# A decoder layer's prologue with half sums of v and z ahead of the whole sums of q and k, and the gate rows made on VectorE alone

## The reference

```python
h = x * (1.0 + scale[:, None, :]) + shift[:, None, :]      # scale, shift, gate = silu(c) @ w_ada + b_ada
proj = h @ w_in + b_in        # sb_q, sb_k, sb_v, sb_z | ml_q, ml_k, ml_v, ml_o, ml_z, ml_i, ml_f | g_sb, g_ml
y_sb = stick_breaking_attention(sb_q, sb_k, sb_v)          # 8 heads of 64
y_sb = (y_sb * silu(sb_z)) @ w_sb_proj
mq, mk = silu(causal_depthwise_conv([ml_q, ml_k]))
hm = mlstm_chunkwise(mq, mk, ml_v, ml_i, log_sigmoid(ml_f))   # 4 heads of 128
y_ml = (head_norm(hm) * sigmoid(ml_o) * silu(ml_z)) @ w_ml_proj
y = (sigmoid(g_sb) * y_sb + sigmoid(g_ml) * y_ml) @ w_out
return layer_norm(ALPHA * x + (1.0 + gate) * y)
```

## Time and profile before

| | |
|---|---|
| median of 3 runs | 951.34 us |
| profiled execution, whole | 953.3 us |
| its span, first to last instruction | 951.6 us |
| TensorE busy | 924.0 us (97%) |
| VectorE busy | 610.9 us (64%) |
| ScalarE busy | 440.6 us (46%) |
| GpSimd busy | 167.7 us (18%) |
| mean granted TensorE clock | 0.994 |
| chain that ended last: TensorE | 92% |

### The profile page before, as it was taken

How to read it: one execution, slowest core, us unless ns; L and a number is a source line. 1 busy time by engine, 2 the same in 40 slices (tenths; PEclk the granted TensorE clock), 3 DMA queues, 4 the chain that set the end, 5 groups by cost and what they waited for, 6 DMA issues and landing times.

```text
span 951.6 us, 12863 instructions
## 1 busy us (share of the span) xinstructions
PE 924.0 (97%) x4958; PEld 756.9 (80%) x4958; DVE 610.9 (64%) x1057; ACT 440.6 (46%) x719; POOL 167.7 (18%) x118
## 2 busy tenths in 40 slices
PE   4899999999999999999999999999999999999996
PEld 3667888888888888888888888888888888878885
DVE  5838886756976748966659867534653333345997
ACT  2544766543676544665446665525742222243100
POOL 1020132230322310232311322302100000002210
PEclk9899999999999999999999999999999999999998
DMA  9921211112211113111122111127712121215232
GB/s 272 335 44 34 67 34 34 34 46 67 67 30 38 25 55 100 24 45 34 34 68 66 45 34 35 34 56 246 228 46 56 45 55 46 89 44 188 89 133 88
DMA packets 90392, 73.95 MB, mean 78 GB/s; under 512 B 4664, under 2 KB 81592, under 8 KB 90332
## 3 DMA queue, kind: packets, MB, share of 16 engines
q1 hardware_dynamic: 85380, 58.32, 22.4%
q0 software_dynamic: 2496, 8.47, 2.7%
q10 hardware_dynamic: 2456, 6.34, 1.8%
HBM read 64.59 MB, written 8.40 MB: 77 GB/s over the span
## 4 chain that ended last, share of the span: by engine, by line
PE 92%; DMA 3%; DVE 3%; SPq 1%; ACT 1%; issue 1%; DVEq 0%; ACTq 0%
PE bank L668 49%; PE bank L646 9%; PE bank L647 9%; PE bank L648 9%; PE bank L817 4%; PE bank L805 3%; DMA a_raw<-in_w_ada 2%; PE bank L792 2%; PE bank L775 2%; PE bank L794 1%; PE bank L793 1%; PE bank L829 1%; PE bank L836 1%; PE bank L840 1%; PE bank L843 1%
## 5 line engine op out<-in xcount | busy, mean ns | idle before, releaser
L668 PE MATMUL bank<-hH,wH 128*128 128x512 f32 x688 | 271.3, 394 | 3.0 <-DVE wL L1443 1.7
L668 PE MATMUL bank<-hL,wH 128*128 128x512 f32 x688 | 271.1, 394 | 0.0
L668 PE MATMUL bank<-hH,wL 128*128 128x512 f32 x688 | 271.0, 394 | 0.0
L606 POOL TENSOR_TENSOR ez<-ez,rem 128x512 f32<-128x512 f32 x72 | 134.6, 1882 | 392.5 <-DVE rem L1629 392.5
L1443 DVE SCALAR_TENSOR_TENSOR wL<-w_raw,wH 128x512 fp32r<-128x512 f32 x116 | 99.2, 859 | 109.6 <-ACT wH L1001 108.4
L668 PEld LDWEIGHTS bank<-hH,wH 128*128 128x128 f32 x688 | 129.2, 188 | 32.9 <-issue 3.7
L668 PEld LDWEIGHTS bank<-hH,wL 128*128 128x128 f32 x688 | 129.3, 188 | 28.8 <-issue 2.9
L668 PEld LDWEIGHTS bank<-hL,wH 128*128 128x128 f32 x688 | 129.3, 188 | 28.5 <-issue 2.9
L1001 ACT ACTIVATE wH<-w_raw 128x512 fp32r<-128x512 f32 x116 | 72.5, 627 | 103.7 <-PE bank L648 70.6
L1629 DVE TENSOR_TENSOR_SCAN rem<-rem,ones 128x512 f32<-128x512 f32 (+2 forms) x96 | 99.9, 1092 | 31.7 <-ACT rem L1108 31.7
L1096 ACT ACTIVATE ez<-bank 128x512 f32<-128x512 f32 x72 | 39.1, 596 | 99.8 <-PE bank L794 99.8
(11 more groups left out here) (260 smaller groups left out, 1483.6 us busy)
## 6 DMA issues: line engine op xcount, KB each, us to landing
w_raw<-in_w_in SPq DMA_DIRECT2D x104, 256.0 KB, 2.9
a_raw<-in_w_ada SPq DMA_DIRECT2D x12, 512.0 KB, 7.2
raw<-in_w_ada POOLq DMA_DIRECT2D x8, 512.0 KB, 5.3
x_in<-in_x SPq DMA_DIRECT2D x8, 512.0 KB, 4.1
out_y<-res SPq DMA_DIRECT2D x7, 512.0 KB, 2.9
x_rows<-in_x SPq DMA_DIRECT2D x3, 1024.0 KB, 10.4
raw<-in_w_out SPq DMA_DIRECT2D x10, 256.0 KB, 4.4
next_vg<-in_w_ada SPq DMA_DIRECT2D x4, 512.0 KB, 7.7
```

Of the source, the lines that this page charges most:

```text
L606: g.tensor_tensor(e, e, r, ALU.mult).then_inc(a_done[h], 1)
L668: ins = t.matmul(banks(number)[half][:], w, a, start=(r == 0), stop=(r == JOB_MM // 2 - 1))
```

## The change

The order of work in the prologue is another, in these parts:

- TensorE takes tiles 0 to 3 of h for v and z (`early`) instead of q and k. ScalarE copies the four half sums from PSUM to `part` (the place of the adaLN buffer 0), ahead of its `shifted(4)`. Then TensorE takes tiles 0 to 3 for q and k (`lower`; three of the four pieces ahead of `gate_rows(4)`), tiles 4 to 7 for q and k, and at last tiles 4 to 7 for v and z (`late`). VectorE adds bias and `part` to the late half sums (`whole_sum`) in its own order between the gates' steps. The chunks of weights are loaded in the order of `PRO`.
- The gate rows are built by VectorE without `r_e`; ScalarE takes exp(-m) straight from `r_m`.
- ScalarE casts kH and qH in the prologue, VectorE makes kL and qL there. In head 0 sig comes from `next_g` (`first_gate`), behind the evacuation of the first half of the first projection.
- `gate_columns` stands behind the scores of s = 0 of head 0; the copies into `tok` and `dec` (`token_columns`) and the columns of the head made from them (`head_tokens`) stand behind the second convolution sum of head 0.
- Buffers are laid out in another order in SBUF.

```diff
 PRE = 48
-PRO_K = 3
-PRO_CHUNKS = 2 * PRO_K
+PRO = [("if", 0), ("v", 0), ("z", 0), ("if", 1), ("q", 0), ("k", 0), ("q", 1), ("k", 1), ("v", 1), ("z", 1)]
+PRO_NAMES = ["if", "q", "k", "v", "z"]
+KH = KT // 2
 A_BUFS = 4
 BLOCKS = [[0], [1], [2, 3], [4, 5], [6, 7]]
...
@@ -659,7 +666,7 @@
                     if half == 0 and term == 0 and k % 4 == 0:
                         pe.wait_ge(wL_done, first + (k // 4 + 1))
                     if r == 0:
-                        pe.wait_ge(drained[half], number - other_banks)
+                        pe.wait_ge(drained[half], number - (1 if number == PRO_JOBS else other_banks))
                     if r == 0 and number == J_GATES + 1:
                         pe.wait_ge(at_out[half], NH * NS)
                     slot = (slot0 + k // 4) % 3
...
+                pe.wait_ge(wL_done, g + 1)
+                return [z[:, pro_slot(g)] for z in (w_proH, w_proL)] if name in "qk" else [z[:, g % 3] for z in (wH, wL)]
+            def pro_product(name, half, k, first, kt):
+                w = [z[:, k % KH] for z in pro_weights(name, k // KH)]
+                return split_product(pro_banks[name][half][:], w, (hH[:, k, halves(half)], hL[:, k, halves(half)]),
+                                     k - first, kt)
+            def early(k, names):
                 pe.wait_ge(hL_done, k + 1)
-                g = PRO_K * (k // 4) + n
-                if k % 4 == 0:
-                    pe.wait_ge(wL_done, g + 1)
-                w = [z[:, pro_slot(g), k % 4] for z in (w_proH, w_proL)]
+                for name in names:
+                    for half in range(2):
+                        ins = pro_product(name, half, k, 0, KH)
+                        if k == KH - 1:
+                            ins.then_inc(part_filled, 1)
+            def lower(name, half):
+                pe.wait_ge(part_drained, 2 * "qk".index(name) + half + 1)
+                for k in range(KH):
+                    pro_product(name, half, k, 0, KT)
+            def tile_of(k, name):
+                pe.wait_ge(hL_done, k + 1)
                 for half in range(2):
-                    ins = split_product(pro_ps[n][half], w, (hH[:, k, halves(half)], hL[:, k, halves(half)]), k, KT)
+                    ins = pro_product(name, half, k, 0, KT)
                     if k == KT - 1:
                         ins.then_inc(filled[half], 1)
+            def late(name):
+                for half in range(2):
+                    pe.wait_ge(drained[half], PRO_NAMES.index({"v": "q", "z": "k"}[name]) + 1)
+                    for k in range(KH, KT):
+                        ins = pro_product(name, half, k, KH, KH)
+                    ins.then_inc(filled[half], 1)
             def gate_columns():
                 pe.wait_ge(q_exp, 3)
+                pe.wait_ge(tok_done, 2)
                 for n in range(2):
                     pe.wait_ge(m_drained[n], M_PRO[n] - 1)
...
-            for n in range(PRO_K, PRO_JOBS):
-                project(0, 0, JOB_MM, base_job=n, other_banks=1 if n == PRO_K else 0)
-            gate_columns()
+            early(0, "v")
+            ada_columns(1)
+            early(0, "z")
+            gate_rows(0)
+            turn_x(2)
+            ada_columns(2)
+            early(1, "vz")
+            turn_x(3)
+            early(2, "vz")
+            gate_rows(2)
+            ada_columns(3)
+            turn_x(4)
+            early(3, "vz")
+            turn_x(5)
+            lower("q", 0)
+            lower("q", 1)
+            lower("k", 0)
+            gate_rows(4)
+            ada_columns(4)
+            turn_x(6)
+            lower("k", 1)
+            turn_x(7)
+            for name in "qk":
+                tile_of(4, name)
+            gate_rows(6)
+            for name in "qk":
+                tile_of(5, name)
+            for name in "qk":
+                tile_of(6, name)
+                tile_of(7, name)
+            pe.sem_inc(w_first_used, PRO_JOBS)
+            late("v")
+            late("z")
...
@@ -877,6 +930,8 @@
                         weighted_values(i, s - 3)
                         weighted_values(i, s - 2)
                     scores(i, s)
+                    if i == 0 and s == 0:
+                        gate_columns()
                     project(i, start, middle)
                     if s > 0:
...
@@ -1036,9 +1090,18 @@
             for d in range(KT):
                 shifted(d)
                 if d == 3:
-                    for g in range(3, PRO_CHUNKS):
+                    for g in range(3, 6):
                         pro_split(g)
-            for g in range(PRO_CHUNKS, PRO_CHUNKS + 3):
+                    act.wait_ge(ada_summed, BLOCK_OF[d + 1] + 1)
+                    for n, name in enumerate("vz"):
+                        for half in range(2):
+                            act.wait_ge(part_filled, 2 * n + half + 1)
+                            a.activation(part_of(name, half), pro_banks[name][half][:], ACT.Copy)\
+                                .then_inc(part_drained, 1)
+                if d == 5:
+                    for g in (6, 7):
+                        pro_split(g)
+            for g in (8, 9):
                 pro_split(g)
             act.wait_ge(params_made, 1)
...
+            act.wait_ge(bias_in, 16)
+            act.wait_ge(rows_zero, 5)
+            bias_copy(r_if[0:2 * NH, halves(0)], 0, 0, r_bias[0:2 * NH, :], pro_ps[0][0])
+            act.wait_ge(if_moved, 2)
+            bias_copy(r_if[0:2 * NH, halves(1)], 1, 0, r_bias[0:2 * NH, :], r_if[0:2 * NH, halves(1)])
+            def pair_copy(name, dst):
+                n = PRO_NAMES.index(name)
...
-                    act.wait_ge(rows_in, 16 * 4)
-                    a.activation(r_e[:], r_f[:], ACT.Exp, scale=-1.0).then_inc(f_ln, 1)
-                    act.wait_ge(f_ln, 1)
-                    a.activation(r_e[:], r_e[:], ACT.Ln, bias=1.0).then_inc(f_ln, 1)
-                if n == 3:
-                    for q in range(1, 4):
-                        r = slice(32 * q, 32 * q + 32)
-                        act.wait_ge(q_rows, q)
-                        a.activation(r_q[r, :], r_q[r, :], ACT.Exp).then_inc(q_exp, 1)
+                    bias_copy(dst[:, halves(half)], half, n, cols[:, 4 * (n - 1):4 * (n - 1) + 1],
+                              pro_banks[name][half][:])
+            pair_copy("q", next_q)
+            act.wait_ge(rows_in, 16 * 4)
+            a.activation(r_e[:], r_f[:], ACT.Exp, scale=-1.0).then_inc(f_ln, 1)
+            act.wait_ge(f_ln, 1)
+            a.activation(r_e[:], r_e[:], ACT.Ln, bias=1.0).then_inc(f_ln, 1)
+            pair_copy("k", next_k)
+            pro_split(10)
+            for half in range(2):
+                act.wait_ge(drained[half], PRO_NAMES.index("k") + 1)
+            a.activation(kH[:], next_k[:], ACT.Copy).then_inc(pair_split, 1)
+            a.activation(qH[:], next_q[:], ACT.Copy).then_inc(pair_split, 1)
+            pro_split(11)
+            for q, (src, scale) in enumerate([(r_m, -1.0), (r_q, 1.0), (r_q, 1.0)]):
+                r = [slice(64, 96), slice(32, 64), slice(96, 128)][q]
+                act.wait_ge(q_rows, q + 1)
+                a.activation(r_q[r, :], src[r, :], ACT.Exp, scale=scale).then_inc(q_exp, 1)
+            def first_gate():
+                for half in range(2):
+                    act.wait_ge(drained[half], PRO_JOBS)
+                    a.activation(sig[:, halves(half)], next_g[:, halves(half)], ACT.Exp, scale=-1.0)\
+                        .then_inc(sig_exp, 1)
             def odds(i, s):
...
@@ -1236,9 +1305,13 @@
                     conv_exps(i, 0)
             def iteration(i, last):
                 segs, _ = segments()
+                if i == 0:
+                    tasks(i, -1, 24, last)
+                    first_gate()
                 act.wait_ge(sig_capped, i * 2 + 1)
                 a.activation(sig[:], sig[:], ACT.Ln, bias=1.0).then_inc(sig_log, 1)
-                tasks(i, -1, 24, last)
...
-            for g in range(3, PRO_CHUNKS):
+            for g in range(3, 6):
                 pro_split(g)
...
             ada_rows(4, KT // 2, KT)
             low_h(5)
+            for g in (6, 7):
+                pro_split(g)
             mod_columns(4)
             low_h(6)
             low_h(7)
-            for g in range(PRO_CHUNKS, PRO_CHUNKS + 3):
+            for g in (8, 9):
                 pro_split(g)
...
-                link.mark(v.tensor_tensor(bm[:], r_b[:], r_m[:], ALU.subtract))
-                link(v.tensor_tensor(r_e[:], r_i[:], r_b[:], ALU.subtract))
+                dve.wait_ge(b_scanned, 1)
+                dve.wait_ge(q_rows, 1)
+                v.tensor_tensor(bm[:], r_b[:], r_m[:], ALU.subtract).then_inc(bm_made, 1)
+                dve.wait_ge(bm_made, 1)
                 by = lambda z: z.rearrange("p (c t) -> p c t", t=P)
-                v.tensor_copy(r_q[0:32, :], r_e[0:32, :]).then_inc(tok_done, 1)
                 r = slice(32, 64)
```

(73 more changed lines are left out.)

135 lines of the change are left out of this document (49 added, 86 removed).

## The result

The changed kernel takes 954.69 us (median of 7 runs, 952.14 to 956.17) against 951.34 us before: a ratio of 1.0031 with a 95% interval of 1.0021 to 1.0040. It is slower by 0.35%, 3.35 us; the interval lies above the 1.9 us (0.2%) that the prediction took for what a measurement can tell.

What follows compares the result with a forecast made beforehand. TensorE was taken to bound the kernel: its place in head 0 comes 1.8 us later through VectorE's backlog, plus 1.1 us half clock, so 951.34 + 2.9 = 954.2 us; range 949.9 to 957.0.

Steps and rivals of the forecast that it cites:

- What bounds the kernel: TensorE is full after the prologue, so moving its place in head 0 by x us moves the end by x.
- the half clock behind the new wait: Behind the 3.6 us idle at next_v's transposes, part of a half-clock stretch: 1.1 us, between 0 and 1.66.
- The exchanged wait: At `turn_x(5)`, a wait behind ScalarE's copies replaces the old 1.8 us wait: TensorE idle about 1.4 + 0.2 us.
- The clock behind it: Behind the wait at `turn_x(5)`, TensorE's half clock costs 1.66 us as before (bounds 0 and 1.66).
- rival 2: Clock stays up behind ScalarE's copies, chain starts 1.66 us earlier: 951.5 us, or 952.6 with the later drop; chance 0.25.
- The matmuls ahead of `turn_x(7)`: In the prologue, 36 more matmuls stand ahead, so `turn_x(7)` starts at 60.4 instead of 54.88, 5.5 us later.
- The chain of the gates: From `turn_x(7)` to VectorE's row logs takes 17.0 us, so these start at 77.4 instead of 72.49.
- VectorE's sum: VectorE's operations from the row logs at 77.4 to the first copy of `token_columns` in head 0 end at 108.2.
- TensorE's waits: Into head 0, TensorE waits for chunk 13 from 101.5 to 103.0, then idles 3.6 us for `tok` until 108.2.
- Rival 1: VectorE does not set the end in head 0, TensorE passes unstopped: 948.1 us, or 946.5 with clock up; chance 0.17.
- Rival 3: VectorE's backlog goes on behind next_v's transposes and TensorE waits again, adding 1 to 3 us: 955 to 957; chance 0.12.
- My lead for that chunk: Chunk 15's split, done at 116.4 before the change and used about 117.7, is 1.3 us ahead of need.

Runs made afterwards that it cites:

- the repeated run: The changed kernel itself, unchanged, run again beside the kernels with added VectorE work: 954.48 us.
- k_behind: Changed kernel with the lower products of k each one place later, behind the transposes of h tiles 6 and 7: 953.43 us, ratio to before 1.0018.
- the padding: Two or four extra 128x1024 VectorE additions in head 0: before + two 951.64 us; changed + two 955.89 and 955.95; changed + four 957.66.
- tok_first: Changed kernel with token_columns and head_tokens ahead of VectorE's caps and second convolution sum in head 0: 951.68 us, ratio to before 0.9998.
- turn_late: Changed kernel with the transposes of next_v in head 0 behind the 21 matmuls that followed them: 951.55 us, ratio to before 0.9997.
- all_four: Changed kernel with ScalarE's copies behind shifted(4), token_columns and head_tokens ahead of the first caps, and gate_rows(6) and turn_x(7) earlier on TensorE: 947.24 us.
- changed + four: Changed kernel with four more 128x1024 additions on VectorE ahead of the head's columns in head 0: 957.66 us.
- changed + two, again: Changed kernel with two more 128x1024 additions on VectorE ahead of the head's columns in head 0, second time: 955.95 us.
- gates_first: Changed kernel with lower k half 0 behind turn_x(6), lower k half 1 and tile 4 of k behind gate_rows(6): 951.46 us, ratio to before 0.9991.

## Why the prediction was right, point by point

The forecast was 951.34 + 2.9 = 954.2 us, and 954.69 was measured. The path (gates later, VectorE's chain, a wait for `tok`) is as told, and the experiments bear it out. That the profiled execution meets the sum to 0.4 us at each mark from `turn_x(7)` on (60.21, 77.02 and 107.85 against 60.4, 77.4 and 108.2) is in part luck, by the two errors at the clock below.

**What bounds the kernel**: right. After the change TensorE is busy again to the last tenth from 112 us on (588.00 of 588.00 us up to 700 in the repeated run), as it was from 91 on before. And in the profiled executions of the kernel before and of the changed one the time from the transposes of next_v to the end was 951.6 - 106.43 = 845.2 and 954.4 - 107.85 = 846.6 us; the 1.4 us between them go back to the half clock behind the new wait (forecast 1.1, within 0 to 1.66). At the ninth matmul behind the transposes it has cost 1.64 us (107.85 to 112.19, against 106.43 to 109.13 before); 0.26 of these are gone at the end.

**The exchanged wait**: right. `turn_x(5)` waited 1.45 us for ScalarE, whose four copies stood ahead of it (forecast 1.4), and moving them gave 1.5 us back.

**The clock behind it**: wrong, and made good by a second error. I put 1.66 us there for a half clock; the clock was full (1.00 from 45.0 to 48.7). But the block ahead of it, whose 38.98 I took over from the trace of before, started at 40.55, because this execution had half clock from about 27 to 33.6 us, where the trace of before has it from about 28 to 31.5. The two errors are nearly equal in size (1.66 and 1.57 us), so `turn_x(7)` came out at 60.21 (forecast 60.4) for a wrong reason: that was luck. With the full clock at the wait and the start of the trace of before, my own sum is that of rival 2, 951.5 to 952.6. Two steps failed: the 1.66 us, and the assumption that the prologue ahead of a change keeps its times. Nothing in its order differs, yet its clock does from one execution to the next. The condition of rival 2, the clock staying up behind ScalarE's copies, was met in the profiled execution, one of the longest; its time fits only the shortest (952.14, with a mean clock of 0.998, against 0.993 in those of 956.1 and 956.2). That page of the Trainium skill (TensorE: Matmul & The Clock Gate, "Why this matters for your kernels") was borne out at this wait, which is shorter than the gaps it warns of, and not at 28 us, where the clock was 0.50 behind a wait of 2.1 us, nor in the trace of before, where it fell behind one of 1.36 us.

**The matmuls ahead of `turn_x(7)`**: the sum is right, its reason miscounted. 24 more stand there, not 36: of the 36 lower products ahead of `gate_rows(4)` 12 stand in the place of tile 4, which stood there before, and the fourth lower block stands in the place of tile 5. The sum of blocks had it so: 24 matmuls at 0.24 us are 5.7 us, near the 5.5 forecast.

**The chain of the gates**: right. Row logs 16.8 us behind `turn_x(7)` (forecast 17.0), at 77.02 (77.4). I had named `gate_rows(6)` as done in time; it was, with 0.8 us to spare (the row logs came 13.0 us behind it, and 12.2 in k_behind, where it was the later root), which the first reordering used up at once.

**VectorE's sum**: right in total, 30.83 us against 30.8, with terms that differ: two half sums with PSUM took 1.33 us from start to start, not 1.2 (84.09 to 85.42; inside its bounds of 1.2 and 1.5); the memsets and the head's columns 0.8 us, not 1.1. `row_columns` as reckoned: two subtractions on 32 partitions in 2.47 us. Building r_q without r_e saved nothing. The first scores, which I called six pairs of matmuls, are six matmuls (three rows of two), and took the 0.94 us from 96.07 to 97.01 (forecast 0.9).

**TensorE's waits**: 0.4 for the sum of v (forecast 0.6), 0.8 for chunk 13 (1.5), 3.1 for `tok` (3.6); a little smaller each. About 0.16 us of that is how it is counted: the profile shows idle time from a matmul's end, 0.39 us behind its start, and I reckoned from its spacing of 0.23. At chunk 13 TensorE came 0.35 us later than I had it, and at `tok` the copy came sooner (VectorE reached it 30.55 us behind the row logs, not 30.8, and these started at 77.02, not 77.4).

**Rival 1** (VectorE is not the end of it) fell with the wait for `tok` in the trace, with the padding and with the reordered gates. **Rival 3** (backlog goes on) did not come in the changed kernel, but in tok_first and turn_late, where TensorE was set free ahead of it: 0.94 and 1.04 us at chunk 15. My lead for that chunk, 1.3 us, was too small: I left out the eight transposes of `turn_weights(0)` between the scores and its first use. With them the use lies near 118.7 before the change and the lead was 2.3 us. That is also a part of why tok_first waited 0.94 and not 3 us there: with the transposes and at the times of the changed kernel the use is near 116.2, not 115, which takes 1.2 us off; the rest is that TensorE, held by two other waits, reached its transposes 27.6 us behind the row logs, not 26.9.

## What to carry to other kernels

Filling a wait of the bounding engine with work taken from later gains only if nothing that others build on stands behind the filling: here 24 more matmuls that nobody was waiting for went ahead of the last tile of h, which came 5.3 us later for it, and the chain of 17 + 31 us over ScalarE, DMAs and VectorE that starts there then ended 3.1 us behind TensorE's need. Put the work that feeds the longest chain on other engines first, and use the free work to fill behind it. And when a consumer's input is moved from an idle stretch of an engine into its queue (here the copy into `tok`, 16 us ahead of its use before), the new arrival time is that queue's, to be summed operation by operation; moving only that input forward uncovers the next one in the same queue.

## What the runs showed of the hardware that I had not expected

- The same instructions in the same order had granted TensorE clocks of 0.93, 0.96 or 1.00 between 17 and 64 us, in different executions, with the start of the row logs at 77.0, 75.5 and 74.6 us. That is 2.4 us of scatter before anything else; the range of the changed kernel is 4.0 us. That all_four scatters by 0.4 us in five runs may be because little is left in it that waits; no run shows this.
- The length of a wait did not tell what the clock would be behind it. In the prologue these two waits, the first in the kernel before, the second in the changed one, each ahead of eight transposes and eight matmuls of one column, were followed by half clock, until about 31.5 and 33.6 us:

```profile
26.13 1.10 PE L702 MATMUL bank<-ident,x_rows 128*128 128x128 f32 x8 [1.36 <-DMA x_rows<-in_x]
...
26.32 1.50 PE L709 MATMUL bank<-ident,x_rows 128*128 128x128 f32 x8 [2.09 <-DMA x_rows<-in_x]
```

  At the same place waits of 1.01 us (changed + four) and 1.02 us (changed + two, again) were followed by 1.00 and by 0.69 between 28.0 and 33.5 us. A wait of 1.45 us ahead of the eight transposes of `turn_x(5)` was followed by a full clock. In head 0 the 3.1 us wait at 108 was followed by 0.63 over 3.7 us, which cost 1.4 us by the end, and the 2.2 us wait of gates_first by a full clock. What decides is open.
- Half clock costs nothing where TensorE waits anyway. The second execution with two additions had its idle time in three parts (1.1, 2.1 and 1.6 us) and the same mean clock between 100 and 112 us as the unpadded one beside it, 0.86, yet only 953.8 - 108.77 = 845.0 us to the end: its slow matmuls stood ahead of the wait for `tok`.
- The product of next_vg and sig on VectorE (128x1024) took 2.24 us while POOL was multiplying, where a subtraction of that shape takes 1.22 to 1.23. All four products of the trace stood beside a product of POOL, so that POOL is the cause is not shown.
